# Expert routing with the router's weights as the fixed operand and ranks from comparisons made at once; a sum of squares moved from the output stage into the scan before it

## What is computed

```python
scores = jax.nn.sigmoid((t @ router_w).astype(jnp.float32))
sel = scores + router_b.astype(jnp.float32)
grouped = sel.reshape(-1, N_EXPERT_GROUPS, EXPERTS_PER_GROUP)
group_score = lax.top_k(grouped, TOP_K)[0].sum(-1)
g_idx = jnp.argmax(group_score, axis=-1)
...
_, local = lax.top_k(in_group, TOP_K)
expert_idx = g_idx[:, None] * EXPERTS_PER_GROUP + local
wts = jnp.take_along_axis(scores, expert_idx, axis=1)
wts = wts / jnp.sum(wts, axis=-1, keepdims=True)
```

## Time and profile before

| | us |
|---|---|
| runs | 2446.78, 2455.73, 2455.8 |
| median | 2455.73 |
| profiled execution | 2447.53 |
| its span, first to last instruction | 2445.8 |
| PE busy in the span | 2157.8 (88%) |
| DVE busy | 1683.1 (69%) |
| ACT busy | 1364.0 (56%) |
| mean granted clock of PE | 0.936 |

### The profile page before, as it was taken

One profiled execution on the slowest core, in us unless ns is written; L12 is line 12 of the kernel. 1 busy time (PEld: TensorE's weight loads), 2 busy tenths in 40 slices (PEclk: granted clock), 3 DMA queues, 4 the chain that ended last, 5 costly groups with the idle time before them and its releaser, 6 DMA issues. The chain is left out here.

```text
span 2445.8 us, 36362 instructions
## 1 busy us (share of the span) xinstructions
PE 2157.8 (88%) x12334; PEld 1774.6 (73%) x12334; DVE 1683.1 (69%) x2848; ACT 1364.0 (56%) x2135; POOL 276.9 (11%) x357
## 2 busy tenths in 40 slices
PE   4999899989998999968897699996689996799993
PEld 4899876679995666756566588785578886677782
DVE  5884636278555688987653599996547864699993
ACT  2663414266454355675433478885367852688882
POOL 0000000000000265556000011011000000010100
PEclk8999999999999999988998699998799987899996
DMA  6555431546543766500021499998122221699991
GB/s 223 164 182 177 143 107 53 176 163 199 173 147 114 265 217 236 212 10 1 26 78 43 173 379 385 390 390 310 54 93 70 69 87 61 253 400 392 394 364 70
DMA packets 127255, 454.98 MB, mean 186 GB/s; under 512 B 13824, under 2 KB 17792, under 8 KB 126976
## 3 DMA queue, kind: packets, MB, share of 16 engines
q1 hardware_dynamic: 116160, 413.14, 46.8%
q0 software_dynamic: 10944, 39.85, 4.3%
HBM read 431.97 MB, written 20.97 MB: 185 GB/s over the span
## 5 line engine op out<-in xcount | busy, mean ns | idle before, releaser
L2722 DVE TENSOR_TENSOR moe_w_lo<-ring,moe_w_hi 128x1024 fp32r<-128x1024 f32 x384 | 462.5, 1221 | 62.4 <-ACT moe_w_hi L2660 57.4
L2660 ACT CAST moe_w_hi<-ring 128x1024 fp32r<-128x1024 f32 x384 | 399.0, 1049 | 148.1 <-PE ps L236 120.2
L373 DVE TENSOR_TENSOR ffn_w_lo<-ring,ffn_w_hi 128x1024 fp32r<-128x1024 f32 x132 | 160.9, 1222 | 99.7 <-ACT ffn_w_hi L325 99.5
L234 PE MATMUL ps<-moe_w_hi,moe_own 128*128 128x512 f32 x512 | 214.2, 418 | 12.1 <-DVE moe_own L2729 11.1
L235 PE MATMUL ps<-moe_w_lo,moe_own 128*128 128x512 f32 x512 | 205.1, 401 | 0.0
L236 PE MATMUL ps<-moe_w_hi,moe_own 128*128 128x512 f32 x512 | 204.8, 400 | 0.0
L325 ACT CAST ffn_w_hi<-ring 128x1024 fp32r<-128x1024 f32 x132 | 137.4, 1044 | 106.0 <-PE ps L236 106.0
L234 PE MATMUL ps<-ffn_h_hi,ffn_w_hi 128*128 128x256 f32 x608 | 173.3, 285 | 11.1 <-DVE ffn_w_lo L373 11.1
L235 PE MATMUL ps<-ffn_h_lo,ffn_w_hi 128*128 128x256 f32 x608 | 172.0, 283 | 0.0
L236 PE MATMUL ps<-ffn_h_hi,ffn_w_lo 128*128 128x256 f32 x608 | 172.0, 283 | 0.0
L234 PE MATMUL ps<-even_h_hi,even_w_hi 128*128 128x512 f32 x320 | 131.9, 412 | 11.9 <-DVE even_h_lo L1771 9.3
(11 more groups left out here) (542 smaller groups left out, 5630.4 us busy)
## 6 DMA issues: line engine op xcount, KB each, us to landing
ring<-in_weights SPq DMA_DIRECT2D x766, 512.0 KB, 5.4
expert_rows<-moe_y POOLq DMA_DIRECT2D x32, 512.0 KB, 7.2
token_rows<-moe_token_rows SPq DMA_DIRECT2D x6, 512.0 KB, 2.6
sq<-in_cmp_w SPq DMA_DIRECT2D x1, 2048.0 KB, 8.0
both<-in_x SPq DMA_DIRECT2D x1, 1024.0 KB, 5.8
both<-in_context SPq DMA_DIRECT2D x1, 1024.0 KB, 8.1
out<-both SPq DMA_DIRECT2D x1, 1024.0 KB, 4.8
cols<-in_cols SPq DMA_DIRECT2D x1, 720.5 KB, 9.1
```

Source lines behind the costliest of these rows:

```text
L234: pe.matmul(out, w_hi, x_hi, start=start, stop=False)
L373: dve.tensor_tensor(w_lo[:, u % WB], k.ring[:, (first + u) % RING], w_hi[:, u % WB], ALU.subtract).then_inc(w_split, 1)
L2660: act.copy(w_hi[:, j % WB].rearrange("p h f -> p (h f)"), k.slot(act, first + GU + j, e).rearrange("p a f -> p (a f)")).then_inc(w_rounded, 1)
L2722: dve.tensor_tensor(w_lo[:, j % WB].rearrange("p h f -> p (h f)"), k.ring[:, (first + GU + j) % RING].rearrange("p a f -> p (a f)"), w_hi[ ...
```

## The change

Routing. (1) The router's weights are the fixed operand (128x16) and 512 (or 256) tokens move; each feature tile's product waits for its own pieces of h only. The sigmoid is taken on 16 partitions x tokens (`across`), and PE transposes it back, 128 tokens at a time, into bank 5, where DVE reads the scores. (2) Ranks come from a helper `ranks`, which writes for each member of a group which others beat it, without a drain between the comparisons, and sums them up once; it is used in each group, then on the group scores, which are the sum of the two best. The tiles it fills are cleared ahead of the wait for the scores. (3) The places are summed by one product of the triangle with all tiles and tt_n - 1 products with ones shifted by a tile, raised as `placed`; the counts go to another bank and have their own semaphore `counted`, for which DVE waits after the place work. (4) DVE copies the scores out of PSUM after `chosen`.

Output stage. (5) The squares of `zs` are made by ACT at the end of the scan's list, each behind its gate, into a tile of the scan that is no longer used; PE sums them behind its last scan product, in bank 6. (6) In `even_out` PE starts with the 8 products of the mean, then the first output tile; ACT rounds `zs` only, and takes the root without waiting. Banks 4 and 5 serve for mean and centred squares. In `ssd`:

```diff
+        z_squares = xs_tok[:, :, :].rearrange("p t f -> p (t f)").rearrange("p (m t) -> p m t", m=KD)
...
+                pe.wait_ge(added, NU - 1)
+                for t in range(KD):
+                    pe.wait_ge(z_squared, t + 1)
+                    pe.matmul(k.ps[:, Z_BANK, :], k.ones[:, :], z_squares[:, t, :], start=(t == 0), stop=(t == KD - 1))
...
+                for m in range(KD):
+                    act.wait_ge(z_gated, m + 1)
+                    act.activation(z_squares[:, m, :], zs[:, m, :], ACT.Square).then_inc(z_squared, 1)
...
-                        dve.tensor_tensor(zs[:, m, :], y[:, m, :], zs[:, m, :], ALU.mult)
+                        dve.tensor_tensor(zs[:, m, :], y[:, m, :], zs[:, m, :], ALU.mult).then_inc(z_gated, 1)
```

In `even_out`:

```diff
-                for t in range(3):
-                    mean(t)
                 for t in range(KD):
-                    pe.wait_ge(z_squared, t + 1)
-                    mm = pe.matmul(k.ps[:, Z_BANK, :], k.ones[:, :], k.sq[:, t, :], start=(t == 0), stop=(t == KD - 1))
-                    if t == KD - 1:
-                        mm.then_inc(z_summed, 1)
-                    if 3 <= t < KD - 1:
-                        mean(t)
-                    elif t == KD - 1:
-                        mean(t).then_inc(mean_done, 1)
+                    mm = pe.matmul(k.ps[:, MEAN_BANK, :], k.ones[:, :], cf[:, t, :], start=(t == 0), stop=(t == KD - 1))
+                mm.then_inc(mean_done, 1)
+                for t in range(KD):
                     part_of(0, t, (zs_hi, zs_lo), z_split)
...
-                    act.activation(k.sq[:, t, :], zs[:, t, :], ACT.Square).then_inc(z_squared, 1)
                     act.activation(zs_hi[:, t, :], zs[:, t, :], ACT.Copy, scale=gain[:, t:t + 1]).then_inc(z_rounded, 1)
-                act.wait_ge(z_summed, 1)
```

In `moe_route`, PE:

```diff
-                pe.wait_ge(ready, KD * len(segs))
+                for t in range(KD):
+                    pe.wait_ge(ready, (t + 1) * len(segs))
+                    mm = pe.matmul(k.ps[0:EXPERTS, 6, 0:n], router_w[:, t, :], k.h[:, t, 0:n], start=(t == 0), stop=(t == KD - 1))
+                mm.then_inc(routed, 1)
+                pe.wait_ge(scored, 1)
                 for tt in range(tt_n):
-                    for t in range(KD):
-                        mm = pe.matmul(k.ps[:, 6, tt * EXPERTS:(tt + 1) * EXPERTS], k.h[:, t, tt * P:(tt + 1) * P],
-                                       router_w[:, t, :], start=(t == 0), stop=(t == KD - 1))
-                mm.then_inc(routed, 1)
+                    mm = pe.transpose(k.ps[:, 5, tt * EXPERTS:(tt + 1) * EXPERTS], across[:, tt * P:(tt + 1) * P],
+                                      k.ident[0:EXPERTS, 0:EXPERTS])
+                mm.then_inc(score_turned, 1)
...
-                for tt in range(tt_n):
-                    for s in range(tt + 1):
-                        pe.matmul(k.ps[:, NORM_BANK, tt * EXPERTS:(tt + 1) * EXPERTS], k.upto[:, :] if s == tt else k.ones[:, :],
-                                  chosen[:, s, :], start=(s == 0), stop=(s == tt))
+                picks = chosen[:, :, :].rearrange("p t e -> p (t e)")
+                mm = pe.matmul(k.ps[:, NORM_BANK, 0:tt_n * EXPERTS], k.upto[:, :], picks, start=True, stop=False, skip_group_check=True)
+                for s in range(1, tt_n):
+                    mm = pe.matmul(k.ps[:, NORM_BANK, s * EXPERTS:tt_n * EXPERTS], k.ones[:, :], picks[:, 0:(tt_n - s) * EXPERTS],
+                                   start=False, stop=(s == tt_n - 1), skip_group_check=True)
+                mm.then_inc(placed, 1)
                 for s in range(tt_n):
-                    mm = pe.matmul(k.ps[:, NORM_BANK, tt_n * EXPERTS:(tt_n + 1) * EXPERTS], k.ones[:, :], chosen[:, s, :],
-                                   start=(s == 0), stop=(s == tt_n - 1))
-                mm.then_inc(placed, 1)
+                    mm = pe.matmul(k.ps[:, 6, 0:EXPERTS], k.ones[:, :], chosen[:, s, :], start=(s == 0), stop=(s == tt_n - 1))
+                mm.then_inc(counted, 1)
```

ACT:

```diff
-                act.activation(score[:, :, :, :].rearrange("p t g e -> p (t g e)"), k.ps[:, 6, 0:tt_n * EXPERTS], ACT.Sigmoid
-                               ).then_inc(scored, 1)
+                act.activation(across[:, :], k.ps[0:EXPERTS, 6, 0:n], ACT.Sigmoid).then_inc(scored, 1)
```

DVE; the 47 operations between the bias and `picked` (L2449 to L2485) give way to:

```diff
+                def ranks(to, of, wins, many):
+
+                    for i in range(many):
+                        own = of[:, :, i:i + 1]
+                        if i:
+                            dve.tensor_tensor(wins[:, :, i, 0:i], of[:, :, 0:i], own.broadcast_to([P, of.shape[1], i]), ALU.is_ge)
+                        if i + 1 < many:
+                            dve.tensor_tensor(wins[:, :, i, i + 1:], of[:, :, i + 1:], own.broadcast_to([P, of.shape[1], many - i - 1]),
+                                              ALU.is_gt)
+                    dve.drain()
+                    dve.tensor_reduce(to, wins, AX.X, ALU.add)
+                    dve.drain()
+
+                dve.memset(beaten[:, :, :, :, :], 0.0)
+                dve.memset(g_beaten[:, :, :, :], 0.0)
+                dve.wait_ge(score_turned, 1)
...
+                ranks(r4, v4, b4, EPG)
+                dve.tensor_scalar(r4, r4, TOPK - 0.5, None, ALU.is_lt)
                 dve.drain()
+                tt_(b4[:, :, 0, :], r4, v4, ALU.mult)
+                dve.tensor_reduce(g_score[:, :, :].rearrange("p t g -> p (t g)"), b4[:, :, 0, :], AX.X, ALU.add)
                 dve.drain()
+                ranks(g_rank[:, :, :], g_score[:, :, :], g_beaten[:, :, :, :], EGROUPS)
+                dve.tensor_scalar(g_rank[:, :, :], g_rank[:, :, :], 0.5, None, ALU.is_lt)
                 dve.drain()
...
+                tt_(c4, r4, g_rank[:, :, :].rearrange("p t g -> p (t g)").unsqueeze(2).broadcast_to([P, G, EPG]), ALU.mult)
                 dve.sem_inc(picked, 1)
+                dve.tensor_copy(score[:, :, :, :].rearrange("p t g e -> p t (g e)"), turned_scores)
+                dve.drain()
...
+                dve.wait_ge(counted, 1)
+                dve.tensor_reduce(top[:, 0, 0:1], k.ps[:, 6, 0:EXPERTS], AX.X, ALU.max)
```

More of the change, by code:

```diff
@@ L1885, in ssd @@
                               "rows_made", "decayed", "dt_abs", "dt_log", "late_scaled", "late_added", "rows", "expd", "mixed",
-                              "summed", "added", "xdt_made", "xw_made", "faded") as sems, \
+                              "summed", "added", "xdt_made", "xw_made", "faded", "z_gated", "z_squared") as sems, \
                 nc.Block(name="ssd", no_gpsimd_drain=True) as block:
             (a_ready, la_ready, cleared, turned, kept, sums, across, rounded, ended, rows_made, decayed, dt_abs, dt_log, late_scaled,
-             late_added, rows, expd, mixed, summed, added, xdt_made, xw_made, faded) = sems
+             late_added, rows, expd, mixed, summed, added, xdt_made, xw_made, faded, z_gated, z_squared) = sems
             def heads(ap):
@@ L2166, in _ @@
                 late_taps(len(pieces))
+MEAN_BANK, C_BANK, Z_BANK = 4, 5, 6
 def even_out(k, x, col, zs, cf, gate, late):
@@ L2199, in _ @@
             def _(pe):
-                def mean(t):
-                    return pe.matmul(k.ps[:, MEAN_BANK, :], k.ones[:, :], cf[:, t, :], start=(t == 0), stop=(t == KD - 1))
                 def part_of(n, t, parts, split):
@@ L2380, in moe_route @@
         sel = sb("sel", [P, tt_n, EGROUPS, EPG])
-        w3 = sb("w3", [P, 8, tt_n * EGROUPS])
+        beaten = sb("beaten", [P, tt_n, EGROUPS, EPG, EPG])
+        g_beaten = sb("g_beaten", [P, tt_n, EGROUPS, EGROUPS])
+        g_score, g_rank = sb("g_score", [P, tt_n, EGROUPS]), sb("g_rank", [P, tt_n, EGROUPS])
+        across = sb("across", [EXPERTS, n])
         rank = sb("rank", [P, tt_n, EGROUPS, EPG])
         top = sb("top", [P, 4, tt_n])
-        with stage_semaphores(nc, f"{name}_route", *NORM_SEMS, "made", "ready", "routed", "scored", "picked", "placed",
-                              "turned", "kept", "rows_stored") as sems, nc.Block(name=f"{name}_route", no_gpsimd_drain=True) as block:
-            norm, (made, ready, routed, scored, picked, placed, turned, kept, rows_stored) = sems[:4], sems[4:]
+        with stage_semaphores(nc, f"{name}_route", *NORM_SEMS, "made", "ready", "routed", "scored", "score_turned", "picked",
+                              "placed", "counted", "turned", "kept", "rows_stored") as sems, nc.Block(name=f"{name}_route", no_gpsimd_drain=True) as block:
+            norm, (made, ready, routed, scored, score_turned, picked, placed, counted, turned, kept, rows_stored) = sems[:4], sems[4:]
             UNITS, BANKS = 2 * tt_n, 4
@@ L2441, in _ @@
                 r4 = rank[:, :, :, :].rearrange("p t g e -> p (t g) e")
-                wk = [w3[:, i, :] for i in range(8)]
+                b4 = beaten[:, :, :, :, :].rearrange("p t g i j -> p (t g) i j")
                 def tt_(o, a, b, op):
@@ L2446, in tt_ @@
                     dve.drain()
```

(27 more changed lines are left out.)

20 lines of the change are left out of this document (2 added, 18 removed).

## The result

| | before | changed |
|---|---|---|
| median of four runs, us | 2455.72 | 2410.7 |
| lowest and highest | 2446.78, 2455.8 | 2403.16, 2412.04 |
| profiled execution | 2447.53 | 2410.38 |
| its span | 2445.8 | 2408.6 |
| PE busy | 2157.8 (88%) | 2147.7 (89%) |

The ratio is 0.9826 with a 95% interval of 0.9805 to 0.9846, so 43 us less (38 to 48). The forecast was 2405, in 2397 to 2421, and the sum's gain 44.1.

What follows compares the result with a forecast made beforehand. PE was taken to set the pace except where chains of small steps keep it waiting. Gains of 20.7 + 12.9 + 10.5 = 44.1 us took 2447.5 to 2403.4, put at 2405 for unexplained slower executions; range 2397 to 2421.

Steps and rivals of the forecast that it cites:

- the sum: Whole kernel: gains of 20.7, 12.9 and 10.5 us add to 44.1, taking 2447.5 to 2403.4.
- What bounds the kernel: Whole kernel: PE sets the pace except in chains of small steps; a microsecond saved in a routing is the kernel's.
- Router product: First routing, PE: earlier start on tiles of h, clock rising after 4.0 us; DVE adds the bias 9.4 us earlier.
- Ranking: First routing, DVE: 20 instructions instead of 48, twelve comparisons largely undrained; 4.0 us against 12.4, so 8.4 less.
- Queue order and placement: First routing, PE: token transposes end by 1341.3 to 1343.3, about when chosen is there; placement 3.4 us cold, 1.7 warm.
- the cold case: First routing's placement with PE at the half clock: 16 instructions in 3.4 us, then a DVE and PE tail of 0.55.
- The stores: First routing's end: token rows' stores are late next, landing 1344.4 to 1345.2; the routing ends 1345.2, 20.7 us gain taken.
- the 5 us that were named as a sign of being wrong: Either routing: the prediction is wrong if DMA sets the end later than 5 us after chosen.
- Second routing: 256 columns: scores 3.8 us earlier, ranking 8.1 less, end 2067.5 instead of 2080.82; 12.9 us taken (10.5 to 14).
- Squares' sums: Scan and output stage: squares' products move into the scan, so the second sum of squares starts 10.5 us earlier.
- the 1190 named as a sign: End of the scan: the prediction is wrong if the scan's last products run past 1190 us.
- The share put on the reciprocal: Output stage, second and third tile: the earlier reciprocal leaves 0.3 of 2.95 us waiting for split weights.

Runs made afterwards that it cites:

- the kernel with the late root: Changed kernel with the output stage's first-norm root held back until PE finished the first output tile; 2411.92 us in one execution.
- the drains: Changed kernel with a DVE drain after each ranking comparison, ten added in all; 2408.45 us in one execution.
- the later profile of the same kernel: Changed kernel unaltered, run again for comparison on another chip; median 2406.17 us (2403.15 to 2417.19), second routing 15.4 us.
- the products of ones: Changed kernel with six unread products of ones on PE ahead of the first routing's router product; 2408.01 us in one execution.

## Why the prediction was right, point by point
**What bounds the kernel.** Right: each stretch handed on what it saved (the stretches between are within 2.0 us of before). The premise that no DMA is waited for held for weights; the token rows' stores came to be last in both routings.

**Router product.** Right in the mechanism and in the price: the start is 5.6 us earlier (5.7 in the sum), and the new form is cheaper in the first routing only as the clock rises under it. The rise was taken at 4.0 us; in the profile it came at 5.9, in the kernel with the late root at about 2.8, so scores came 8.6 us earlier (12.05 against 20.68) or 10.2, for 9.4 in the sum. The 9.4 lies between two outcomes of the clock, and which of them a run gets was luck.

**Ranking.** It took 3.65 us, for 4.0 in the sum; the reduction over 256 elements took 0.42, for some 0.5 (0.26 to 0.30 and 0.2 more) in the sum.

**Queue order and placement.** The transposes ended before `chosen` (PE waited 0.35 us for it), paced by ACT's copies, which took 4.01 us for the 4.1 expected. The placement and DVE's tail were done 2.6 us behind `chosen`, less than the 3.9 of the cold case, and hidden behind the stores.

**The stores.** Right that they are late next: as the drains show, 2.0 us of DVE's chain are hidden behind them. The prediction had both end at much the same time (the stores at 1344.4 to 1345.2, DVE at 1343.8 to 1345.5); the last store landed 1.7 us behind DVE's end (1344.42 against 1342.69). That is 4.3 us behind `chosen`, not far from the 5 us that were named as a sign of being wrong. The routing's gain was 19.9 for 20.7, and the clock and the stores are the difference.

**Second routing.** The gain was 14.0 us for 12.9, since the clock was up from the start; in the later profile of the same kernel, where it was down, 11.7.

**Squares' sums.** The gain to the second sum of squares was 10.5 us for 10.5, and the terms came out too: 7.03 us in the scan, an end 1.1 us behind the late taps (1.2 in the sum), means at the full clock, waits for split weights down from 2.5 to 0.2. The scan's last products ended at 1196.25, or 1189.9 less the 6.4 us by which everything there was later, just inside the 1190 named as a sign. The share put on the reciprocal held after the correction for the overshoot (an estimated 2.6 for 2.65). "From there the chain is the old one" held but for the +2.0 us up to the first routing's h.

**The sum** of gains was 44.1, measured 44.4 in the changed stretches, but that close an agreement is luck in part: the first routing gave 0.8 us less, by the clock and the stores, the second 1.1 more, by the clock, and in the later profile of the same kernel the second gave 1.2 less. The 8 us between executions, which the prediction could not explain, it took for two levels. They are a spread: with 6.4 us against it in the unchanged part the profiled execution came out at 2410.4, and the lowest run, 2403.16, at the 2403.4 of the sum. The 2405 was too near the low end. A sum made against one execution inherits that execution's luck, and this one had the earliest last gate of the thirteen (1184.2). From the median of before, 2455.72, the same 44.1 gives 2411.6, and 2410.7 was measured.

## What to carry to other kernels
Before pricing a chain of small steps, find the piece of it that can start on part of its input: here a product that takes its moving operand tile by tile starts 5.6 us earlier, of which 4.6 arrived at the scores, and its shape gave another 4.0, only since the clock rose under it. On DVE, results that do not need each other can share one drain; ten spared drains were 1.7 us. And ask of every shortened chain what ends next: here it was the stores of another engine's side product, 2.0 us behind.

## What the runs showed of the hardware that I had not expected
The granted clock in stages that no edit touches differs from execution to execution, and its cost adds up: 7.2 us over the first 1190 us of thirteen profiles. The same 16 router instructions on 256 columns took 3.63 us, 6.32 and 6.55; those on 512 columns 7.04 after the products of ones, and otherwise 8.33 to 9.96. An edit of less than some 5 us in this kernel is to be judged by the stage's own length in the trace, at a like clock, and not by the whole.
